# Whole experts per block in the ranked fetches, and output columns in the last four blocks of the first experts

## The reference

```
aff = softmax(h @ w_router); vals, idx = top_k(aff per expert, 32)
xs = h[idx]
hid = silu(einsum('becd,edf->becf', xs, w_gate)) * einsum('becd,edf->becf', xs, w_up)
y = einsum('becf,efd->becd', hid, w_down) * vals
x = x + mod * scatter_add(y); x = rmsnorm(x)
```

```
for g in range(4):
    h = silu(einsum('td,edf->tef', t, w_gate[g])) * einsum('td,edf->tef', t, w_up[g])
    y = y + einsum('tef,efd->td', h * gate[:, g, :, None], w_down[g])
x = layer_norm(ALPHA * x + y)
```

## Time and profile before

| | |
|---|---|
| median of 3 runs | 1617.17 us (1615.1 to 1618.91) |
| profiled execution, its own time | 1616.84 us |
| its span, first to last instruction | 1615.1 us |
| PE busy | 1344.6 us (83%) |
| DVE, ACT busy | 482.2 us (30%), 297.7 us (18%) |
| moved by DMA | 492.62 MB, mean 305 GB/s |
| DMAs from `ranked_d` | 240 of 512 KB, 24 of 1024 KB |
| DMAs from `ring_d` of a whole slot | 156 of 2048 KB |

### The profile page before, as it was taken

How to read it: one execution, slowest core, us unless ns; L and a number is a source line. 1 busy time by engine, 2 the same in 40 slices (tenths; PEclk the granted TensorE clock), 3 DMA queues, 4 the chain that set the end, 5 groups by cost and what they waited for, 6 DMA issues and landing times. The chain is left out here.

```text
span 1615.1 us, 18893 instructions
## 1 busy us (share of the span) xinstructions
PE 1344.6 (83%) x7496; PEld 747.6 (46%) x7496; DVE 482.2 (30%) x1128; ACT 297.7 (18%) x617; POOL 0.2 (0%) x4
## 2 busy tenths in 40 slices
PE   6999999956665656599999999866999989998658
PEld 4665877412211211166767743321567677433213
DVE  5125553101101101014664522210246744322102
ACT  2422202100000000012332312200223223122002
POOL 0000000000000000000000000000000000000000
PEclk9999999978878878799999999997999999999889
DMA  9465478999999999992421499999915214899994
GB/s 392 165 253 208 159 292 329 399 428 427 428 428 427 428 428 428 428 425 78 191 105 53 164 396 391 410 409 408 388 53 209 86 71 157 343 401 409 409 407 193
DMA packets 63297, 492.62 MB, mean 305 GB/s; under 512 B 7008, under 2 KB 7392, under 8 KB 39008
## 3 DMA queue, kind: packets, MB, share of 16 engines
q1 hardware_dynamic: 63056, 491.15, 74.9%
q10 hardware_dynamic: 144, 0.13, 0.0%
HBM read 490.21 MB, written 1.05 MB: 304 GB/s over the span
## 5 line engine op out<-in xcount | busy, mean ns | idle before, releaser
L659 PE MATMUL PS<-A 128*128 128x256 f32 (+5 forms) x1568 | 367.5, 392 | 5.3 <-DMA A<-ring_d 1.6
L1015 PE MATMUL PS<-A 128*32 128x512 f32 x1536 | 234.2, 747 | 140.1 <-DMA A<-ring_d 140.1
L659 PEld LDWEIGHTS PS<-A 128*128 128x128 f32 (+1 forms) x1568 | 274.3, 193 | 90.1 <-issue 51.0
L1540 PE MATMUL PS<-A 128*32 128x512 f32 (+1 forms) x1024 | 168.0, 628 | 41.1 <-DMA A<-ranked_d 32.9
L1015 PEld LDWEIGHTS PS<-A 128*32 128x32 f32 x1536 | 52.5, 125 | 308.6 <-issue 239.6
L1569 PE MATMUL PS<-A 128*32 128x512 f32 (+1 forms) x512 | 93.9, 713 | 31.6 <-issue 31.6
L1540 PEld LDWEIGHTS PS<-A 128*32 128x32 f32 (+1 forms) x1024 | 48.1, 123 | 143.9 <-issue 143.3
L2096 DVE TENSOR_TENSOR A<-A,PS 128x512 f32<-128x512 f32 x8 | 5.5, 688 | 322.7 <-PE PS L1015 322.7
L664 PE MATMUL PS<-A 128*128 128x128 f32 (+1 forms) x396 | 58.4, 278 | 18.2 <-DVE A L2096 7.1
L664 PEld LDWEIGHTS PS<-A 128*128 128x128 f32 (+1 forms) x396 | 44.7, 144 | 56.0 <-issue 31.0
L1569 PEld LDWEIGHTS PS<-A 128*32 128x32 f32 (+1 forms) x512 | 25.9, 137 | 96.0 <-issue 95.4
(11 more groups left out here) (392 smaller groups left out, 1277.8 us busy)
## 6 DMA issues: line engine op xcount, KB each, us to landing
A<-ring_d SPq DMA_DIRECT2D x156, 2048.0 KB, 26.3
A<-ranked_d SPq DMA_DIRECT2D x240, 512.0 KB, 14.7
A<-ranked_d SPq DMA_DIRECT2D x24, 1024.0 KB, 8.4
A<-ring_d SPq DMA_DIRECT2D x2, 1312.0 KB, 22.2
A<-ring_d SPq DMA_DIRECT2D x2, 1280.0 KB, 22.4
A<-p_d SPq DMA_DIRECT2D x1, 1232.0 KB, 22.6
A<-xT_d SPq DMA_DIRECT2D x1, 1024.0 KB, 5.3
A<-cT_d SPq DMA_DIRECT2D x1, 1024.0 KB, 11.8
```

The costliest lines, as they stand in the source:

```text
L659: ins = g.matmul(out, l, r, start=n == 0, stop=n == len(pairs) - 1)
L1015: ins = g.matmul(ps[32 * e:32 * e + 32, :], rows_of(kk, e), wv[:, kk % 2, e, :], start=kk == 0, stop=kk == 7)
L1540: ins = g.matmul(ps[m * s:m * s + m, :], XS2[u % 2][:, kk, c:c + m], wv[:, kk % nk, s, :], start=kk == 0, stop=kk == 7)
```

## The change

Two parts. **Whole experts:** a `gr` block now holds gate and up of one expert (4096 floats a partition, one DMA) in place of two rows kk of four experts (four DMAs of 1024 floats) or four rows kk of two experts. A `dr` block of a four-expert unit holds two experts whole (two DMAs of 2048 floats) in place of one of the two inner rows of four experts (four DMAs of 1024). `whole_experts` waits for all `gr` blocks of the unit, does the same matmuls in the same order, and gives all the blocks free behind them. **Output columns:** the last four blocks of `w_down` hold all eight rows kk by 128 output columns each. `last_columns(q)` has 32 matmuls of 128 moving columns in place of 8 of 512, and the chain behind it runs in rows of 128 features. The spare matmuls ahead of the third and fourth block were 2 and 3; now there are 2 ahead of each of them, and 1 and 2 further on.

```
@@ four_experts
-                    if done == ("ye", 3, 1) and part > 1:
-                        keep_on((2, 3)[part - 2], "ye", part)
@@ PE, behind the last half of the first experts
-                        squares(0)
-                        squares(1)
-            combine(3, 2)
-            combine(3, 3)
-            for b in (2, 3):
-                ins = squares(b)
-            ins.then_inc(*full("fsum"))
+            def last_columns(q):
+                w, i = weights("w_down", 3, 1, q)
+                wv = w.rearrange("p (k e n) -> p k e n", k=8, e=4)
+                ps = fresh("ye", 3, 1, q)
+                arrived(i)
+                for kk in range(8):
+                    for e in range(4):
+                        ins = g.matmul(ps[32 * e:32 * e + 32, 0:128], HIDT[:, kk, 32 * e:32 * e + 32], wv[:, kk, e, :], start=kk == 0, stop=kk == 7)
+                ins.then_inc(*full("ye", 3, 1, q))
+                finished(i)
+            def combine_row(d):
+                ps = fresh("ex", 3, d, "row")
+                g.wait_ge(*at("ye", 3, 1, d - 4))
+                g.matmul(ps[:, 0:256], YE[:, 3, d * 128:(d + 1) * 128], PVT[:, 3, :], start=True, stop=True).then_inc(*full("ex", 3, d, "row"))
@@ gate_up of a ranked unit
+            def whole_experts(n, ps):
+                (x, j), u = UNITS[n], gather_of(n)
+                m = 32 if four(n) else 64
+                got = [weights("gr", l, x, j, s) for s in range(128 // m)]
+                wv = [w.rearrange("p (k n) -> p k n", k=8) for w, i in got]
+                for d in range(4):
+                    g.wait_ge(*at("xs2", l, u, d // 2, d % 2))
+                for w, i in got:
+                    arrived(i)
+                for kk in range(8):
+                    for s in range(128 // m):
+                        c = (j % 2) * 128 + s * m
+                        ins = g.matmul(ps[m * s:m * s + m, :], XS2[u % 2][:, kk, c:c + m], wv[s][:, kk, :], start=kk == 0, stop=kk == 7)
+                ins.then_inc(*full("sg", l, n))
+                for w, i in got:
+                    finished(i)
@@ ACT, behind the last half
-            final_squares(2)
-            final_squares(3)
+            for d in range(4, 8):
+                full("ye", 3, 1, d - 4)
+                s.activation(YE[:, 3, d * 128:(d + 1) * 128], bank("ye", 3, 1, d - 4)[:, 0:128], ACT.Copy).then_inc(*out("ye", 3, 1, d - 4))
+                s.wait_ge(*at("ex", 3, d, "row"))
+                s.activation(T[:, d, :], X[:, d, :], ACT.Square, bias=0.0, scale=1.0).then_inc(*out("fsq", d, "row"))
@@ SP, ranked
-                n = SLOT // len(of)
-                c = n * part + (4096 if kind == "dr" else 0)
+                of, n, c = (of[part:part + 1], SLOT, 0) if kind == "gr" else (of[2 * part:2 * part + 2], SLOT // 2, SLOT)
```

More of the change, by code:

```diff
@@ L1079, in combine, with squares @@
                 ins.then_inc(*full("ex", x, b))
-            def squares(b):
-                g.wait_ge(*at("fsq", b))
-                for k in (2 * b, 2 * b + 1):
+            def squares(rows, *key):
+                g.wait_ge(*at("fsq", *key))
+                for k in rows:
                     for ti in range(2):
@@ L1110, in tensor @@
                 g.wait_ge(*at("hidt", x, 1))
-                for half in range(2):
+                for half in range(2 if x < 3 else 1):
                     ps = fresh("ye", x, half)
@@ L1118, in tensor @@
                         banks.hold("fsum")
[L1119 to L1125 removed]
+            def last_columns(q):
[12 more added lines that the diff above has]
+                g.matmul(ps[:, 0:256], YE[:, 3, d * 128:(d + 1) * 128], PVT[:, 3, :], start=True, stop=True).then_inc(*full("ex", 3, d, "row"))
+            last_columns(0)
+            squares((0, 1), 0)
+            last_columns(1)
+            squares((2, 3), 1)
+            combine_row(4)
+            combine_row(5)
+            keep_on(2, "ye", 1)
+            last_columns(2)
+            squares((4,), 4, "row")
+            squares((5,), 5, "row")
+            combine_row(6)
+            keep_on(2, "ye", 2)
+            last_columns(3)
+            squares((6,), 6, "row")
+            keep_on(1, "ye", 3)
+            combine_row(7)
+            keep_on(2, "ex", 3)
+            squares((7,), 7, "row").then_inc(*full("fsum"))
             banks.release("fsum")
@@ L1525, in gate_up @@
                 ps = high("sg", l, n)
[L1526 to L1534, removed]
+                if x:
+                    whole_experts(n, ps)
+                    return
@@ L1535, in gate_up @@
+                for part in range(2):
+                    w, i = weights("gu", l, n, part)
+                    wv = w.rearrange("p (k s n) -> p k s n", k=4, n=512)
+                    for d in (2 * part, 2 * part + 1):
                         g.wait_ge(*at("xs2", l, u, d // 2, d % 2))
                     arrived(i)
[L1537 to L1540, removed]
@@ L1541, in gate_up @@
-                    ins.then_inc(*(full("sg", l, n) if part == parts_ - 1 else up("pe")))
+                    for kk in range(4 * part, 4 * part + 4):
+                        for s in range(2):
+                            c = (j % 2) * 128 + s * 64
+                            ins = g.matmul(ps[64 * s:64 * s + 64, :], XS2[u % 2][:, kk, c:c + 64], wv[:, kk % 4, s, :], start=kk == 0, stop=kk == 7)
+                    ins.then_inc(*(full("sg", l, n) if part else up("pe")))
+                    finished(i)
@@ L1557, in down @@
                 got = [weights("dr", l, x, j, part) for part in range(2 if four(n) else 1)] if x else [weights("dn", l, 2 * n)]
[L1558 to L1561, removed]
+                wd = [w.rearrange("p (e f n) -> p e f n", e=2, f=2) for w, i in got]
                 for w, i in got:
@@ L2107, in vector @@
                     slots(x + 1)
-            for b in range(4):
+            for b in range(2):
                 combine(3, b)
+            for d in range(4, 8):
+                full("ex", 3, d, "row")
+                v.scalar_tensor_tensor(out=X[:, d, :], in0=bank("ex", 3, d, "row")[:, 0:256], scalar=MA[:, 7, d:d + 1],
+                                       in1=X[:, d, :], op0=ALU.mult, op1=ALU.add).then_inc(*out("ex", 3, d, "row"))
             v.wait_ge(*at("fstd"))
@@ L3495, in block @@
             x, half, q = a
+            if (kind, x, half) == ("w_down", 3, 1):
+                w = n[kind][0, 12:16, :, 512 + 128 * q:640 + 128 * q]
+                return w.reshape(4, 8, 128, 128).transpose(2, 1, 0, 3).reshape(128, -1)
             w = n[kind][0, 4 * x:4 * x + 4, 256 * q:256 * q + 256, 512 * half:512 * half + 512]
```

5 lines of the change are left out of this document (3 added, 2 removed).

## The result

The changed kernel takes 1610.72 us, median of 6 runs (1608.01 to 1612.86). The kernel before, run beside it, takes 1617.53 us, median of 6 (1615.1 to 1620.05). The ratio is 0.9958, interval 0.9946 to 0.9971: 6.8 us less, where the prediction had 9.4 (1607.8 us).

What follows compares the result with a forecast made beforehand. Expert stages were taken as bound by transfers, mixers by PE. Gains of 7.4 us at the layers' ends and 2.0 at the first experts' end made 9.4: 1616.84 to 1607.4, median 1607.8, range 1603.3 to 1614.5.

Steps and rivals of the forecast that it cites:

- Part 1: Ranked expert stages: larger packets lift 408 to 427 GB/s, saving 0.23 us per gr block and 0.15 per dr block.
- Part 2: Units 4 to 6: slots come free later, so down(4)'s block and the stream run 2.0 us later in each layer.
- Part 3: Units 8 to 10: one wait of some 10 us, then a gate of 8.4 to 9.9 us that doesn't cut the stream.
- The bound of 11.4: Units 8 to 10: the longest gate, in us, that three more slots in flight allow before the stream is cut.
- The rival of the cold gates: Units 8 to 10: low clock lasts the whole gate, 14.0 us, emptying the DMA engines; 1623.2 us, chance 0.09.
- Part 4: Last down of each layer starts earlier: 3.5 us gained in the first, 3.9 in the second, together 7.4.
- Part 5: End of the first experts: root 5.4 us behind the last landing in place of 7.4, 2.0 us gained.
- The rival of no faster packets: Ranked expert stages: 408 GB/s stays and only the late release's 2.0 us is left; 1617.4 us, chance 0.11.
- that of the useless end: End of the first experts gives nothing, PE falling behind or narrow matmuls slow; 1609.8 us, up to 1614, chance 0.14.
- That of "more": The late release's 2.0 us are hidden, last blocks land 4.95 us earlier; 1603.4 us, chance 0.11.

Runs made afterwards that it cites:

- whole_4k: The changed kernel with each ranked DMA cut into pieces of 1024 floats a partition, same blocks, waits and gates; 1619.53 us, ratio 1.0021.
- pairs_early: The changed kernel with two-expert units 4 and 5 keeping the old gr blocks, each given free behind its 16 records; 1606.59 us, ratio 0.9928.
- pairs_warm: pairs_early with 6, 7, 9 and 16 spare 512-column matmuls ahead of the waits of units 7, 8, 9 and 10; 1612.09 us, ratio 0.9966.
- e0: Not a run: the first of the second block's two expert stages; first matmul to last down 229.3 us before the change, 226.6 after.
- before_again: The kernel before, unchanged, run once more for a second profile; 1618.09 us.
- columns_only: The changed kernel without the whole-expert hunks, so only the output columns in the last four blocks; 1613.86 us, ratio 0.9979 against the kernel before.
- pairs_tail: pairs_early with combine_row(4) ahead of last_columns(1) and no spare matmul ahead of combine_row(7); 1602.88 us, ratio 0.9914.

## Why the prediction was right, and where its sizes were off

**Part 1, the rate, was right.** 424 GB/s. In `e1` the first block of unit 8 landed at 1466.4 + 18.1 = 1484.5 before and at 1458.4 + 23.1 = 1481.5 after, as their rows show:

```profile
L3252 SPq DMA_DIRECT2D A<-ranked_d x1: 947/947/947, 1466.4 to 1466.4; - x1
DMA to landing us min/median/max: 18.1/18.1/18.1
```

```profile
L3299 SPq DMA_DIRECT2D A<-ranked_d x1: 946/946/946, 1458.4 to 1458.4; - x1
DMA to landing us min/median/max: 23.1/23.1/23.1
```

From there to the last landing (1593.5, 1585.8) lie 11 `gr` and 10 `dr` blocks: 109.0 us before, 104.3 after, 4.7 saved, where 11 x 0.23 + 10 x 0.15 = 4.0 was counted. Over six stages of each kind it is 108.7 and 105.0 on the mean, 3.6 saved. whole_4k and the changed kernel differ only in how the ranked DMAs are cut, 408 against 424 GB/s.

The Trainium skill, page "DMA: Bandwidth & Descriptors", section "Specifications", has transfers at line rate from 512 B on; by that the term would have been nothing. The runs do not agree: pieces of 4 KB and of 8 to 16 KB, all far above it, move at rates that differ by 4%.

**Part 2, the late release, was right for unit 5 and left out unit 6.** Counted from the end of the stage's first 12 records (1369.07 and 1363.57), `down(4)`'s block landed after 84.1 us before and after 85.7 now: 1.6 late, 2.0 was predicted. The step that failed is "From there the stream has no gap". From that landing to unit 8's first block it is 31.3 us before and 32.2 now. Between them lie five `gr` blocks (four of unit 7, where the prediction counted three, and the first of unit 8) and `down(5)`'s block, which is cut as before. It should have been shorter by 5 x 0.23 = 1.15, so 2.0 more were lost. The rows put them at unit 6: it too has no wait ahead of it (7.07 us from 1449.04), and all its four slots come free together when it ends at 1456.1, where before its first had come free after a quarter. The two issues around it, and the window behind it:

```profile
L3299 SPq DMA_DIRECT2D A<-ranked_d x2: 332/332/333, 1448.8 to 1456.3; - x2
DMA to landing us min/median/max: 9.4/9.8/10.2
```

```profile
1456.00:1462.00 6.00, 6.00 (x28) 4.00 (x26) 4.18 (x8) 3.77 (x8) 0.00 (x0) 1.00 0.94 360
```

The block issued at 1448.8 lands at 1459.1, the next one, issued at 1456.3, at 1465.7: 6.7 us apart in place of 4.9. No run gives unit 6's slots free one by one, so this cause is read from the rows and not tested.

The sum for `e1` is then -1.6 - 0.9 + 4.7 = 2.2 us for the last landing, against 2.95 predicted. Over the six stages of each kind the means are 1.1 us late at `down(4)`'s block, 0.6 more to unit 8's first, and 2.0 us gained at the last landing. pairs_early gives only the slots of units 4 and 5 free earlier and lands its last block another 1.4 us earlier (1583.6, 220.8 us behind the end of its first 12 records, against 222.2).

**Part 3, the gates, was right in what it decides.** 8.3 to 9.8 us were measured for the predicted 8.4 to 9.9, all below 11.4. The waits were 6.1 to 8.8, and 15.88 for unit 10, where "some 10" was put: less work of PE stands between the gates of units 9 and 10. The longest wait cost no more than the shortest, 8.61 against 9.76 us of gate. The bound of 11.4 was tested from the other side by pairs_warm: there the gate of unit 10 in `e0` ended 12.9 us after its fourth block had landed (at 1111.2), and the DMA share fell to 0.87; in its `e1` the gate ended 10.2 us after the landing and the share behind it was 1.01. So the bound lies between the two. The rival of the cold gates is out: no gate stayed on the low clock to its end.

The Trainium skill, page "TensorE: Matmul & The Clock Gate", section "HAM oscillation — how this bites in real kernels", has tiles begin on the lower clock behind such waits. The rows of units 7 to 10 agree with it for each gate, by 1.3 to 2.7 us. It cost little here, since the transfers set the end: nothing in the stream that the runs can tell, and at most the 0.9 us by which PE was late in one stage of pairs_early.

**Part 4, the ends of the layers.** Predicted 3.5 and 3.9 us. In `e1` PE was free before the last landing, so the last `down` starts 0.1 us behind it; in `e0` it has no wait and starts 0.3 us behind. In the first pair of executions `e0` gained 2.7 and `e1` 5.0, of which 1.7 come from the slow start that before had and after had not. The means of three executions, 2.4 in each layer, are the better measure, so this term was too large by 2.6 in all. Two things are in it. The stream brought 2.0 a layer and not 2.95. And the prediction took PE's lateness at the last `down` (0.7 and 1.2 us in before) for the kernel's: in before_again it is 0.1 and 0.1, in columns_only 0.1 and 1.4, so on the mean of the six 0.6 us, and what can be gained there is 0.5.

**Part 5, the end of the first experts.** 2.0 predicted, 2.4 measured, but in two pieces. `last_columns` takes 1.95 us (2.1 predicted). The root came 6.0 and not 5.4 us behind the landing, since PE reached the last block 0.8 us late and not 0.3: ACT squares row 4 ahead of its copy for row 5, `combine_row(5)` and the third block queue behind that copy (1.5 us late), and the last block behind the third. pairs_tail moves row 4 out of the way, and the root is at 4.9. On the other side 0.9 came that was not counted: the matmuls behind the root take 3.69 in place of 4.28 us and begin 1.9 in place of 2.2 us behind it.

**The sum.** 9.4 predicted, 8.8 between the profiled executions, 6.8 between the medians. The prediction took one execution of before for its sizes, and a part of the lateness of PE that it meant to remove at the ends of the layers was that execution's. The profiled execution of after had no slow start and is the fastest of its six. By the means of the traces the sum is 2.4 + 2.4 + 2.4 = 7.2. The layers gave 2.6 less than predicted and the end of the first experts 0.4 more. The rival of no faster packets is out by whole_4k, that of the useless end by columns_only. That of "more", with part 2's loss hidden, fell too (1603.4 against 1610.72); pairs_early shows that 4 to 5 us of it were to be had.

## What to carry to other kernels

When a block is cut otherwise, ask for each consumer whether it waits for its blocks or is late for them. Where it waits, larger packets pay and one wait for four costs little; where it is late, the release sets the stream, and slots that come free together leave the DMA engines short of work (a share of 0.85 and 0.94 at units 5 and 6 here). So choose the cut by unit: here whole experts where PE waits, halves in units 4 and 5 where it doesn't; what a finer cut of unit 6 would give was not tried. Warmth bought with spare matmuls is worth little where the ring covers the cold gate, and it turns into a loss when the spares run so long that the gate ends later than the ring allows.

## What the runs showed of the hardware

A part of TensorE's low clock belongs to the execution and not to the kernel. At the first matmuls of `e0` and `e1` the same 12 records took 4.12 us in 14 of 24 stage starts of the 12 profiled executions (before, after, and the ten of the experiments) and some 5.8 in the other 10, behind the same instructions and the same wait of 0.49 us. In the changed kernel the stage was 1.4 us (`e0`) and 3.2 us (`e1`) longer in the execution that had it (228.0 and 229.6 us from its first matmul to its last `down`, against 226.6 and 226.4). The start itself took 1.7 us longer; why `e1` lost another 1.5 is open, and the two `e1` of before and before_again, both with the slow start, are 1.3 apart as well (231.4 and 230.1). The landing of the first experts' last block differs by up to 3.0 us between executions. A single profile of a kernel of this kind is thus uncertain by some 3 us, which is as much as the terms of this case, and a term should be taken from several.
